# Low parts of split weights in pieces of 512 columns, and two products of the first layers as three passes of high and low parts

## The reference

```
proj = h @ w_in                      # 11 pieces: q, k, v, gate, ranks, d_q, d_k, d_v, gate_a, gate_b
y_a = (norm(gla(q, k, v)) * silu(g)) @ w_a
o_b = merge_heads(rms_norm(diff_attention(dq, dk, dv)) * (1 - lam_init))   # 512 x 512
y_b = o_b @ w_b                                                            # 512 x 1024
merged = sigmoid(gate_a) * y_a + sigmoid(gate_b) * y_b
x = x + g1 * (merged @ w_out)                                              # 512 x 1024
h = modulate(rms_norm(x));  x = x + g2 * moe(h)      # router, 32 experts, 2 of them for each token
```

## Time and profile before

| | |
|---|---|
| median of 3 runs | 3676.68 us (3673.64 to 3678.28) |
| profiled execution | 3665.6 us, span from first to last instruction 3663.9 us, mean TensorE clock 0.923 of full |
| TensorE matmuls busy | 3145.1 us, 86% |
| VectorE, ScalarE, GpSimd busy | 1131.0 us (31%), 963.9 us (26%), 806.6 us (22%) |
| bytes read from DRAM | 653.64 MB, most of it in the experts' stretches at 400 to 409 GB/s |
| subtractions of low parts on GpSimd (L847, L757) | 407.9 us x52 and 180.2 us x22 |

### The profile page before, as it was taken

One profiled execution on the slowest core, in us unless ns is written; L12 is line 12 of the kernel. 1 busy time (PEld: TensorE's weight loads), 2 busy tenths in 40 slices (PEclk: granted clock), 3 DMA queues, 4 the chain that ended last, 5 costly groups with the idle time before them and its releaser, 6 DMA issues. The chain is left out here.

```text
span 3663.9 us, 42396 instructions
## 1 busy us (share of the span) xinstructions
PE 3145.1 (86%) x15027; PEld 2035.5 (56%) x15027; DVE 1131.0 (31%) x2001; ACT 963.9 (26%) x1351; POOL 806.6 (22%) x382
## 2 busy tenths in 40 slices
PE   6998997887885798998798888687999998799999
PEld 4775654333332576564433333464788776578877
DVE  4465413111111456432211111234343303434330
ACT  4324301111111523421111111234333323433331
POOL 3312200111111321120111111320244343024332
PEclk7998997999997899999799999798999999989999
DMA  5214432999997212431799999411132331112232
GB/s 212 69 58 147 142 112 104 400 409 409 409 406 274 92 57 97 151 108 71 299 408 409 409 408 406 165 52 47 47 110 74 93 111 52 47 46 92 81 91 70
DMA packets 289710, 663.67 MB, mean 181 GB/s; under 512 B 20190, under 2 KB 114708, under 8 KB 289552
## 3 DMA queue, kind: packets, MB, share of 16 engines
q1 hardware_dynamic: 271680, 623.43, 45.7%
q0 software_dynamic: 17872, 38.14, 2.9%
HBM read 653.64 MB, written 25.69 MB: 185 GB/s over the span
## 5 line engine op out<-in xcount | busy, mean ns | idle before, releaser
L869 PE MATMUL psum<-s_parts 128*128 128x512 f32 (+1 forms) x3744 | 956.9, 407 | 96.1 <-ACT s_units L2068 37.6
L869 PEld LDWEIGHTS psum<-s_parts 128*128 128x128 f32 (+1 forms) x3744 | 724.6, 195 | 292.6 <-ACT s_units L2068 45.9
L869 PE MATMUL psum<-s_ring,s_units 128*64 128x512 f32 x3168 | 745.8, 620 | 129.6 <-DMA s_ring<-in_w_expert_in 90.6
L847 POOL TENSOR_TENSOR s_parts<-s_ring,s_parts 128x4096 fp32r<-128x4096 f32 (+2 forms) x52 | 407.9, 7844 | 872.0 <-ACT s_parts L2068 872.0
L869 PEld LDWEIGHTS psum<-s_ring,s_units 128*64 128x64 f32 x3168 | 248.6, 142 | 582.9 <-issue 447.6
L869 PE MATMUL psum<-s_h_low,s_parts 128*128 128x512 f32 (+1 forms) x1872 | 469.9, 391 | 11.2 <-DVE s_hid_low L2039 11.2
L869 PEld LDWEIGHTS psum<-s_h_low,s_parts 128*128 128x128 f32 (+1 forms) x1872 | 350.0, 188 | 95.3 <-DVE s_hid_low L2039 12.1
L869 PE MATMUL psum<-s_units 128*128 (+9 forms) x1520 | 283.6, 401 | 79.9 <-DVE s_gsl L1829 26.7
L757 POOL TENSOR_TENSOR s_parts<-s_ring,s_parts 128x4096 fp32r<-128x4096 f32 (+1 forms) x22 | 180.2, 8190 | 593.4 <-ACT s_parts L2068 593.3
L2068 ACT ACTIVATE s_parts<-s_ring 128x4096 fp32r<-128x4096 f32 (+3 forms) x74 | 237.3, 3210 | 182.3 <-PE psum L869 103.8
L869 PEld LDWEIGHTS psum<-s_units 64*128 64x128 f32 (+3 forms) x1520 | 171.4, 190 | 158.3 <-issue 116.5
(11 more groups left out here) (350 smaller groups left out, 2656.4 us busy)
## 6 DMA issues: line engine op xcount, KB each, us to landing
s_ring<-in_w_expert_in SPq DMA_DIRECT2D x132, 2048.0 KB, 24.0
s_ring<-in_w_expert_out SPq DMA_DIRECT2D x66, 2048.0 KB, 24.9
s_ring<-in_w_in SPq DMA_DIRECT2D x28, 2048.0 KB, 8.6
s_ring<-in_w_ada SPq DMA_DIRECT2D x24, 2048.0 KB, 8.4
s_ring<-in_ffn_w_up SPq DMA_DIRECT2D x40, 1024.0 KB, 6.9
s_ring<-in_ffn_w_down SPq DMA_DIRECT2D x16, 1408.0 KB, 7.0
s_ring<-in_w_out SPq DMA_DIRECT2D x8, 2048.0 KB, 7.9
s_units<-ys_scratch POOLq DMA_DIRECT2D x16, 512.0 KB, 6.3
```

Source lines behind the costliest of these rows:

```text
L847: pool.tensor_tensor(parts[:, s, 0:size], ring[:, s, 0:size], parts[:, 4 + n % 2, 0:size].bitcast(F32), ALU.subtract).then_inc(weights_low ...
L869: return pe.matmul(o, lhsT=lhsT, rhs=rhs, start=start, stop=stop)
```

## The change

**Pieces.** `low_part` in both blocks issues its subtraction in pieces of 512 columns; only the last raises the semaphore. A block of 4096 columns is 8 instructions, one of 2816 is 6, one of 2048 is 4.

**Three passes.** `("yb",)`, `("wo", 0)` and `("wo", 1)` join `SPLIT_A`. The 4 matmuls of a `yb` ticket become 12 fp32r ones, the 8 of a `wo` ticket 24. ScalarE makes `high_part(11)` between the sigmoids of `gb` 3 and 4, `high_part(12)` behind the last sigmoid, `high_part(13)` behind the copies of `mrg`. The activations need parts too: ScalarE copies the normed attention output to fp32r (`dq_hi`, 4 copies) ahead of the sigmoids, and each `mrg[m]` to `h_hi`; VectorE subtracts (`dq_low`, 4; `low_merged`, 8).

**Squares.** The squares for `n2` go to `U` instead of `hT`, since `h_low` lies over `hT`.

**Loads.** Slots 3, 4, 5 are now in use longer: slot 4 until `("wo", 3)`, 3 and 5 until `("wo", 7)`. SyncE's loads of the first two experts are in another order.

```
@@ low_part (first block; the second block alike)
-                pool.tensor_tensor(parts[:, s, 0:size], ring[:, s, 0:size], parts[:, 4 + n % 2, 0:size].bitcast(F32),
-                                   ALU.subtract).then_inc(weights_low_a.sem, weights_low_a.more())
+                for c in range(0, size, 512):
+                    cols = slice(c, min(c + 512, size))
+                    ins = pool.tensor_tensor(parts[:, s, cols], ring[:, s, cols], parts[:, 4 + n % 2, cols].bitcast(F32), ALU.subtract)
+                ins.then_inc(weights_low_a.sem, weights_low_a.more())
@@ SyncE
+        last_of_high = {3: ("wo", 7), 4: ("wo", 3), 5: ("wo", 7)}
-                    sp.wait_ge(TA.done.sem, TA.done_at(l, RA.reader_last(s) if s < 3 else ("gb", 7)))
+                    sp.wait_ge(TA.done.sem, TA.done_at(l, RA.reader_last(s) if s < 3 else last_of_high[s]))
-            for u in (1, 0):
-                expert(l, before * 2, u, u, True)
+            for u, pieces in ((0, (1,)), (1, (1,)), (1, (0, 2)), (0, (2, 0))):
+                expert(l, before * 2, u, u, True, pieces)
@@ TensorE
-            pe.wait_ge(head_normed.sem, head_normed.at(l, 16))
+            w = [...of block_parts(("yb",))]
+            pe.wait_ge(dq_high.sem, dq_high.at(l, HEADS))
+            pe.wait_ge(dq_lowered.sem, dq_lowered.at(l, HEADS))
             for m in range(8):
-                fm(("yb", m), slot_view(RA.slot(("yb",)), 4, D), P * m, dq, 4)
+                o = opened(("yb", m))
+                for n, (a, rows) in enumerate(((0, dq_hi), (1, dq_hi), (0, dq_low))):
+                    for k in range(HEADS):
+                        last = mm(o, w[a][:, k, tok(m)], rows[k], n == 0 and k == 0, n == 2 and k == HEADS - 1)
+                done(last)
             for m in range(KD):
+                if m % 4 == 0:
+                    w = block_parts(("wo", m // 4))
-                if m == 0:
-                    pe.wait_ge(TA.by(("yb", 7)).sem, TA.freed_at(l, ("yb", 7)))
                 o = opened(("wo", m))
-                for k in range(KD):
-                    last = mm(o, wview(RA, ("wo", m // 4), KD, 512)[:, k, tok(m % 4)], mrg[k], k == 0, k == KD - 1)
+                for n, (a, b) in enumerate(TERMS):
+                    for k in range(KD):
+                        if m == 0 and n == 0:
+                            pe.wait_ge(merged_high.sem, merged_high.at(l, k + 1))
+                        if m == 0 and n == 2:
+                            pe.wait_ge(merged_low.sem, merged_low.at(l, k + 1))
+                        last = mm(o, w[a][:, k, tok(m % 4)], h_parts[b][:, k, :], n == 0 and k == 0, n == 2 and k == KD - 1)
@@ VectorE
+            for h in range(HEADS):
+                ve.wait_ge(dq_high.sem, dq_high.at(l, h + 1))
+                ve.tensor_tensor(dq_low[h], dq[:, h, :], dq_hi[h].bitcast(F32), ALU.subtract).then_inc(...)
+            def low_merged(m):
+                ve.wait_ge(merged_high.sem, merged_high.at(l, m + 1))
+                ve.tensor_tensor(h_low[:, m, :], mrg[m], h_hi[:, m, :].bitcast(F32), ALU.subtract).then_inc(...)
             for m in range(8):
                 ...
+                if m:
+                    low_merged(m - 1)
+            low_merged(7)
@@ ScalarE
+            for h in range(HEADS):
+                ae.wait_ge(head_normed.sem, head_normed.at(l, 13 + h))
+                copy(dq_hi[h], dq[:, h, :]).then_inc(dq_high.sem, dq_high.more())
             for m in range(8):
+                if m == 4:
+                    high_part(11)
                 ae.activation(gate_b[m], done(("gb", m)), ACT.Sigmoid).then_inc(...)
+            high_part(12)
+            for m in range(8):
+                ae.wait_ge(TA.by(("yb", m)).sem, TA.freed_at(l, ("yb", m)))
+                copy(h_hi[:, m, :], mrg[m]).then_inc(merged_high.sem, merged_high.more())
+            high_part(13)
```

More of the change, by code:

```diff
@@ L443, in program @@
     mix_parts = h_parts
+    dq_hi = [hid_low[:, 8 + k, :] for k in range(HEADS)]
+    dq_low = [units_high[:, 2 + k, :] for k in range(HEADS)]
     hid_hi = [units_high[:, k, :] for k in range(6)] + [h_low[:, k, :] for k in range(KD)] + [h_hi[:, k, :] for k in range(KD)]
@@ L589, in _, with expert @@
         freed_in_m = (m_in_read[0], m_in_read[1], m_down_made)
-        def expert(l, number, e, u, layer_first):
-            for j in range(3):
+        last_of_high = {3: ("wo", 7), 4: ("wo", 3), 5: ("wo", 7)}
+        def expert(l, number, e, u, layer_first, pieces=range(3)):
+            for j in pieces:
                 s = 3 * u + j
                 if layer_first:
-                    sp.wait_ge(TA.done.sem, TA.done_at(l, RA.reader_last(s) if s < 3 else ("gb", 7)))
+                    sp.wait_ge(TA.done.sem, TA.done_at(l, RA.reader_last(s) if s < 3 else last_of_high[s]))
                     settle(sp)
@@ L780, in _ @@
             small(router_bias_in, rtb[:, 4:36], inp["b_router_expert"][l].partition_broadcast(P))
-            low_part(10)
+            for n in range(10, len(SPLIT_A)):
+                low_part(n)
             for t in range(NT):
@@ L846, in low_part @@
                 settle(pool)
-                pool.tensor_tensor(parts[:, s, 0:size], ring[:, s, 0:size], parts[:, 4 + n % 2, 0:size].bitcast(F32),
-                                   ALU.subtract).then_inc(weights_low.sem, weights_low.more())
+                for c in range(0, size, 512):
+                    cols = slice(c, min(c + 512, size))
+                    ins = pool.tensor_tensor(parts[:, s, cols], ring[:, s, cols], parts[:, 4 + n % 2, cols].bitcast(F32), ALU.subtract)
+                ins.then_inc(weights_low.sem, weights_low.more())
             low_part(0)
@@ L944, in tm_parts, with sumsq @@
                 done(of_parts(o, lambda a, k: h_parts[a][:, k, tok(t)], lambda b, k: w[b][:, k, :]))
-            def sumsq(name, signal, first):
+            def sumsq(name, signal, first, rows=hT):
                 o = opened(name)
@@ L950, in sumsq @@
                     pe.wait_ge(signal.sem, signal.at(l, first + k + 1))
-                    last = mm(o, ones[:], hT[:, k, :], k == 0, k == KD - 1)
+                    last = mm(o, ones[:], rows[:, k, :], k == 0, k == KD - 1)
                 done(last)
@@ L1704, in _ @@
                 head_norm("on", h, 13 + h, dq, sc[:, 6:7], P, on_temps)
+            for h in range(HEADS):
+                ve.wait_ge(dq_high.sem, dq_high.at(l, h + 1))
+                ve.tensor_tensor(dq_low[h], dq[:, h, :], dq_hi[h].bitcast(F32), ALU.subtract).then_inc(dq_lowered.sem, dq_lowered.more())
+            def low_merged(m):
+                ve.wait_ge(merged_high.sem, merged_high.at(l, m + 1))
+                ve.tensor_tensor(h_low[:, m, :], mrg[m], h_hi[:, m, :].bitcast(F32), ALU.subtract).then_inc(merged_low.sem, merged_low.more())
             for m in range(8):
@@ L2084, in done, with squares @@
                 return psum[:, TA.bank(name), :]
-            def squares(first, ready):
+            def squares(first, ready, rows=hT):
                 for k in range(KD):
                     ready(k)
-                    ae.activation(hT[:, k, :], xT[:, k, :], ACT.Square).then_inc(x_squared.sem, x_squared.more())
+                    ae.activation(rows[:, k, :], xT[:, k, :], ACT.Square).then_inc(x_squared.sem, x_squared.more())
             def take_root(name, k, temps=T):
```

12 lines of the change are left out of this document (7 added, 5 removed).

## The result

| | before | after |
|---|---|---|
| median, us | 3675.16 (3666.97 to 3678.28, 4 runs) | 3595.24 (3592.50 to 3597.65, 4 runs) |
| ratio | | 0.9786, 95% interval 0.9774 to 0.9798 |
| profiled execution, span, us | 3665.6, 3663.9 | 3597.65, 3596.0 |
| GpSimd busy, us | 806.6 | 957.5 |

The change makes the kernel 2.1% faster, some 80 us by the medians and 68 by the two profiled executions: the traced execution of the kernel before was 10 us under its median, that of the changed kernel 2 us above. The forecast was 3607, and 3596 in the profiled execution's own time.

What follows compares the result with a forecast made beforehand. TensorE bounds the kernel, except transfers in the experts and VectorE waiting for GpSimd at a few attention gaps. Tail -9.6, loads -4.2, pieces +6.1 and -27.1 make -34.8 per pair of layers, -70 in all: 3607 us, range 3568 to 3650.

Steps and rivals of the forecast that it cites:

- Three passes: `yb` and `wo`: a product costs 0.680 us in place of 0.863, 96 products per layer, -17.6 us per layer.
- The gate gap: Before `gb` 4: ScalarE's copies lengthen TensorE's gap to 8.2 us, +4.8, and a slower clock behind adds +1.1 per layer.
- VectorE in `yb`: VectorE's additions and subtractions in `yb` wait for GpSimd's subtraction and fall behind TensorE: +3 us per layer, bounds 0 and 9.
- Loads: Router to first expert: fewer loads beside the activation stores, so the gather goes earlier: -4.2 us per layer, bounds 0 and -6.
- The pieces' price: Where TensorE waits for GpSimd's subtraction: a block gets 1.9 us longer (0.5 to 2.6), together +6.1 per pair of layers.
- The gains: Attentions and `dn`: VectorE operations wait for one piece's rest instead of a whole subtraction, about -27 us per pair of layers.
- The alternation: Wherever both want the ports: VectorE waits 0.6 us on average for one piece's rest, then GpSimd takes its next piece.
- VectorE always gets in: Rival, at the shared ports: no piece starts while VectorE has a queue; -101 us in all, 3576 us; chance 0.25.
- GpSimd never lets go: Rival, at the shared ports: the next piece goes before the waiting VectorE operation; +15 us, 3691 us; chance 0.07.
- `dn`: Last product of the second block: gain 2 us against 1.4 and 0.9 for longer subtractions, +0.3 per layer.
- Late experts: Rival, first expert: loads from `("wo", 7)` on land late, some 8 us lost per layer, 3631; chance 0.06 with similar slips.
- dear pieces: Rival, feed-forward part: a fixed price of 0.65 us or more a piece makes TensorE wait; about 3700; chance 0.04.

Runs made afterwards that it cites:

- experiment 4: Changed kernel with ScalarE's four copies of the normed attention output moved behind the sigmoids of `gb` 0 to 3: 3583.62 us, ratio 0.9752 to the kernel before.
- experiment 3: Changed kernel with SyncE's loads of the first two experts back in the old order: 3609.31 us, ratio 0.9829 to the kernel before.
- experiment 5: Changed kernel with pieces of 256 columns in place of 512: 3600.53 us, ratio 0.9797 to the kernel before.
- experiment 6: Changed kernel with pieces of 1024 columns in place of 512: 3597.16 us, ratio 0.9790 to the kernel before.
- experiment 7: Changed kernel with one subtraction (n = 2, `gv`) left whole in each layer of the first block: 3577.57 us, ratio 0.9745 to the kernel before.

## Why the prediction was right

The time, the mechanism and the order of the terms came out; the sum came nearer than its terms deserve, since omissions of some 18 us (what the table shows above the priced parts) stood against terms that were too cautious by some 17 (tail 6, loads 4, `dn` 6, attentions 1). That they cancel is luck. So is part of the 70 against 68: by the ratio the change is worth 79 us.

- **Three passes.** Right: 2.72 us a `yb` ticket, 5.44 a `wo` ticket, 0.2267 a matmul, as read from the `gb` tickets. Counting an fp32 matmul as four of them would have given 3 us too much per layer.
- **The gate gap.** The gap of 8.2 was right (8.19), and experiment 4 gives it back. The 1.1 for a slower clock behind it did not come in the changed kernel (5.31 instead of 5.53); behind the same gap it came in experiments 3 and 5 (6.46 to 6.75), so that the term was nothing here is no rule.
- **VectorE in `yb`.** I took +3, with bounds 0 and 9. The gap before `wo` is 1.41 where I had 0.9 without this term: +0.5. Three tickets take 3.4 us and lose 0.7 each against TensorE (forecast: about four of 3.9, losing 1.2), and the others win most of it back. The step that failed is "by the eighth VectorE is some 4 us late": it was 2.1 late at its worst, at the fifth ticket, and 0.65 at the eighth. I let the delay stand instead of letting the slack work it off. This is most of the 3.2 by which the tail was too cautious.
- **Loads.** Forecast -4.2, measured -6.3 and -5.9, at the bound of -6; experiment 3 shows that it is their order. I had the first two stores gain 3 us; the median of all of them gained 3.8.
- **The pieces' price.** 1.0 for eight instead of 1.9: a fixed 0.143 us an instruction. The line through 256 and 4096 columns took 256 at the 0.722 of one that ran alone; in a row they follow each other every 0.69. The line through 2048 and 4096, which pulled the term up, was the worse one. The 17 us that the range gives to pieces at 2.6 don't come out of these terms: 6.1 x 2.6 / 1.9 is 2.2 more per pair of layers, 4.5 in all.
- **The gains.** First-block attention 10.3 and 7.9 for 8.0, second-block 17.6 and 15.4 for 17.1. The alternation was right; an operation behind another one waits for nearly a whole piece, not half of one (1.1, not 0.6), since GpSimd gets its next piece in between the two. The three waiting operations at 290 do what was said of them: 3.2 left, forecast 2.6. The rival that VectorE always gets in is out by experiments 5 and 6, the one that GpSimd never lets go by L2008.
- **`dn`.** Forecast +0.3 with the pieces' price, measured -3.1 and -2.1. The first ticket's run of row by row matmuls went from 23.2 to 20.0 us: 2.6 less idle, and the matmuls behind the old gap no longer slow. The price was 0.3 at `dn` 0 and 0.5 at `dn` 6, not 2.3.
- **What I left out.** The stretch ahead of the first block's attention lost 5.0 and 6.3 us. At `gv` I had priced only the longer subtraction. With it whole the loss is gone (experiment 7). Of it 3.5 us at 160 and 1.6 at 186 are the same matmuls at the other clock level and what hangs on them. No row of before tells which way that falls for a shift of 1 us; a bound of plus and minus 5 us per layer belonged into the sum.
- **Late experts, dear pieces.** Neither came: the first expert's matmuls follow the turn at once, and in the feed-forward part TensorE is busy throughout. But the step "what is won ahead of it is kept" failed in part: the experts' stretches got 1.8 and 4.1 longer, and when experiment 3 took the loads' gain away, they got 1 and 4 shorter again. How is open.

## What to carry to other kernels

Where two engines share an exclusive port, cut the long operation of the one that has slack only where the other was seen to wait; the wait becomes one piece, the price is a fixed sum per instruction, and pieces at a place where somebody waits for their end, and no VectorE operation for the ports, are pure loss (15 us by the ratios at `gv` alone, experiment 7). A copy with a wait, set ahead of work that frees a buffer, costs its wait; look whether it can stand behind. And a kernel whose TensorE clock falls several times per layer can answer a shift of 1 us with 6 us (the second layer at `gv`): undo a small edit, or replace it by an idle operation of the same length, before believing that its gain or loss is its own.

## What was unexpected of the hardware

- A VectorE operation that waits for GpSimd waits for at most one queued instruction: an L2008 of 0.16 us took at most 0.68, 1.22, 2.21, 8.73 us for 256, 512, 1024, 4096 columns. Beside each other both advance by turns.
- L1708 works on 2 numbers per partition and takes up to 1.23 us; L1714, the same kind of operation on 1 number, never waits (212 to 215 ns in 32 cases), not even at 290.84, in the middle of the pieces for which L1708, L1715 and L1716 wait. The Trainium skill (VectorE: DVE Perf Modes, Mode 2×_2P) says that an operation with one tensor in SBUF uses both read ports where the outermost dimension of more than one element is even, or odd and the same in source and destination; the trace agrees for the 2 numbers of L1708. For a single number that rule says nothing, and the trace shows no wait.
- GpSimd's fp32 subtractions in a row cost 0.143 us each above their columns (1.0 for eight instead of one).
- One more GpSimd instruction of 1.29 us in each of two layers cost, with all that followed, 15 us (0.0042 of 3673). 60 us behind it TensorE's granted clock was 0.50 over 4 us instead of 0.87; some of the difference in the clock is older than the instruction, so how much of it is its own is not shown.
